# Sharing the low-part subtraction of weight units 4 to 14 between VectorE and GpSimd in a two-layer encoder kernel

## The chip, the cores and the metric

One core of one Trainium2 chip runs the whole kernel in one launch. The metric is the time of that launch in device microseconds: lower is better. Weights, inputs and constants start in HBM, and the result ends there.

## What is computed

Two layers (`DEPTH = 2`) of an encoder block on x of 256 tokens by 1024 channels, float32:

```
h = RMSNorm(x);  z = h @ W_in              # 1024 x 6656: q, k, v of A and B, pool channels, gates
A = grouped-query attention (8 query heads, 2 key heads, 64 wide), QK norm, axial rotary
B = dilated window attention (12 heads in 3 groups), QK norm, rotary
C = centred mean pooling of 4 channel groups, a linear map per group
x = x + W_o( sum_i sigmoid(gate_i) * P_i(branch_i) )
x = x + (silu(h2 @ W_gate) * (h2 @ W_up)) @ W_down,   h2 = RMSNorm(x),  inner width 2816
```

The kernel keeps nearly float32 precision in products of a reduced-precision float format: each operand is split in a high part (rounded) and a low part (the rest), and a product is hi*hi + lo*hi + hi*lo, three matmuls for each pair of tiles.

## The kernel before

**Weights in units.** All weights of a layer are laid out as a stream of 68 units (`UNITS`). A unit is 1 MB: four k-tiles of 128 rows (`UK = 4`) by 512 columns (`NC`). Units 0 to 25 are W_in, two units for each of 13 column chunks of z; then come the branch projections, W_o, and the feed-forward weights. Four slots (`RING`) of three buffers hold them: `w_raw` (as landed), `w_hi` and `w_lo`.

**A unit's way.** SyncE (line 447) loads unit u into slot u % 4 when TensorE has finished unit u - 4. ScalarE (`split`, line 589) copies `w_raw` to `w_hi`, which rounds it, and raises `unit_hi`. VectorE (`split`, line 752) subtracts, `w_lo = w_raw - w_hi`, over all four k-tiles in one instruction of 2048 columns (line 755), and raises `unit_lo`. Both do this for unit t + 2 at the start of their iteration t. Unit 0 of a layer is split tile by tile (lines 587 and 761).

**TensorE.** For each unit and each of two token tiles (m = 0, 1), `rows` (line 1022) runs eight matmuls with the high part, in pairs (activation high, line 1036, activation low, line 1038), and then four with the low part (line 1047). With m = 0 (`opening`) it waits for `unit_hi` before the first and for `unit_lo` before the low ones; m = 1 waits for neither. Between units and between the two token tiles stand transposes (line 1069), scores (lines 1131 and 1140) and products of probabilities and values (line 1163), by tables written by hand (`TURNS_BEFORE`, `TURNS_WITHIN`, `pair_at`). In unit 0 each high matmul pair and each low matmul has a wait of its own on its k-tile (`first_hi`, `first_lo`).

**VectorE around units 2 to 14.** Iteration t: the maxima of scores (line 868), if any; the split of unit t + 2 (line 755); the scaling of probabilities (line 891), if any; `norm_rotated` of the head region that was rotated one iteration earlier (line 862), which waits for GpSimd's head norms; then `rotate` (lines 830 to 854): the sums of squares for the region (line 830, `head_sums`), and the rotary products and sums. The transposes of queries and keys on TensorE wait for `rotated`, which line 862 raises: those ahead of unit 6 and within it for the first region (two instances of line 862, one per token tile), those ahead of unit 7 for the second, and so on.

**GpSimd around units 2 to 14.** Iteration t of the loop at line 553: `join_probs` (line 512) at t = 12, 14, ..., which waits for the probabilities' transposing DMA, and from the second pair on for TensorE's unit; `head_norm` (lines 485 and 487, a scaling and a power) for the regions of t, which waits for `head_sums`; the loads of gate biases (line 519) from t = 16 on. TensorE's products of line 1163 begin ahead of unit 13 and wait for `join_probs`. In the feed-forward part GpSimd splits hidden values in 16-bit halves and puts them together again (lines 530 and 539).

Of the kernel before, what the change touches and what calls it, by code (L numbers as in the profile page):

```python
# [16 lines left out]
F32 = mybir.dt.float32  # L17
# [3 lines left out]
ALU = mybir.AluOpType  # L21
# [11 lines left out]
UK = 4  # L33
# [8 lines left out]
RING = 4  # L42
# [10 lines left out]
UNITS = U_DOWN + 11  # L53
# [142 lines left out]
POOL_LINKS = 4 + TURNED  # L196


def splits_at(t, ahead=2):

    if t < 2:
        return {2: ([1], [2, 3]), 3: ([1, 2], [3])}[ahead][t]
    return [t + 2] if t + 2 < UNITS else []


def build(nc, x, stream, params, b_gate, eye, angles, pooling, mask, out):
# [3 lines left out]
    with ExitStack() as ctx:  # L210
        def sb(name, shape, dt=F32, to=ctx):
            return to.enter_context(nc.sbuf_tensor(name, shape, dt))

        def sem(name):
            return ctx.enter_context(nc.semaphore(name))
# [17 lines left out]
        w_hi = sb("w_hi", [P, RING, UK, NC], F32R)  # L233
        with ExitStack() as shared:
            w_raw = sb("w_raw", [P, RING, UK, NC], F32, shared)
        w_lo = sb("w_lo", [P, RING, UK, NC], F32R)
# [62 lines left out]
        unit_done = sem("unit_done")  # L299
        unit_hi = sem("unit_hi")  # L300
        unit_lo = sem("unit_lo")
        first_hi = sem("first_hi")
        first_lo = sem("first_lo")
        bank_full = [sem(f"bank_full{b}") for b in range(8)]
# [88 lines left out]
        def probs_room(i):  # L393

            if i < 8:
                return gates[:, i % 2, QK_W:QK_W + NC].bitcast(U16)
            return zqk[:, 1, 1024 + NC * (i % 2):1024 + NC * (i % 2) + NC].bitcast(U16)
# [66 lines left out]
        @block.gpsimd  # L464
        def _(pool):
            def load_gains(layer):
                pool.dma_start(par[:, 0:PR_GAIN], params_v[layer * P:layer * P + P, 0:PR_GAIN]
                               ).then_inc(gains_loaded, 16)

            def load_params(layer):  # L470
                pool.dma_start(par[:, PR_GAIN:PR_W], params_v[layer * P:layer * P + P, PR_GAIN:PR_W]
                               ).then_inc(params_loaded, 16)

            nc.gpsimd.memset(neg_half[:, :, :], -0.5).then_inc(half_ready, 1)
            pool.wait_ge(x1_loaded, 16)
            load_params(0)
            pool.dma_start(rope_c[:, :, :, :].rearrange("p k m d -> p (k m d)"), angles
                           ).then_inc(angles_loaded, 16)

            pool.dma_start(mask_f, mask).then_inc(mask_loaded, 16)  # L480
            pool.wait_ge(half_ready, 1)

            def power(lay, link, dst, src, mul, eps, signal):

                nc.gpsimd.tensor_scalar(dst[1], src, mul, eps, ALU.mult, ALU.add).then_inc(pchain, 1)
                pool.wait_ge(pchain, lay * POOL_LINKS + (link + 1))
                nc.gpsimd.tensor_tensor(dst[0], dst[1], dst[2], ALU.pow).then_inc(signal, 1)  # L487

            def x_norms(lay, which, link):
                pool.wait_ge(x_sums, lay * 8 + 4 * (which + 1))  # L490
                nc.gpsimd.tensor_tensor(sx[:, which, :], ssx[:, 0, :], ssx[:, 1, :], ALU.add  # L491
                                        ).then_inc(pchain, 1)
                pool.wait_ge(pchain, lay * POOL_LINKS + (link + 1))
                power(lay, link + 1, (rstd[:, which, :], sx[:, which, :], neg_half[:, 0, 0:MT]),
                      sx[:, which, :], 1.0 / D, EPS, x_norm)

            def head_norm(lay, n):

                (name, _, hs, first, _, _, _), m = REGIONS[n // MT], n % MT
                mul, eps = (1.0, HD * EPS) if name[2] == "q" else (1.0 / HD, EPS)  # L500
                pool.wait_ge(head_sums, lay * TURNED + (n + 1))
                h = slice(first, first + hs)
                power(lay, 2 + n, (rs[:, m, h], rs_in[:, m, h], neg_half[:, m, h]),
                      ss[:, m, h], mul, eps, head_norms)

            def join_probs(lay, t, i):

                pool.wait_ge(probs_turned[i % 2], 16 * (lay * PAIRS + i // 2 + 1))
                if i >= 2:
                    pool.wait_ge(unit_done, lay * UNITS + RING + t)  # L510
                both = probsT[:, i % 2, :].bitcast(U16).rearrange("p (t h) -> p h t", h=2)
                nc.gpsimd.tensor_copy(both, probs_room(i).rearrange("p (h t) -> p h t", h=2)  # L512
                                      ).then_inc(probs_joined, 1)

            def load_bias(lay, g):
                if g >= 2:
                    for m in range(MT):
                        wait_emptied(pool, lay, (f"z{GATE_CHUNK + g - 2}", m))
                pool.dma_start(bias_sb[:, g % 2, :],
                               gate_v[lay * 6 + g:lay * 6 + g + 1, :].to_broadcast([P, NC])  # L520
                               ).then_inc(bias_loaded[g % 2], 16)

            def hidden_halves(lay, i):

                b = i % 2
                for m in range(MT):
                    wait_emptied(pool, lay, (f"f{i}", m))
                both = hid[:, b, :, :].bitcast(U16).rearrange("p m (f h) -> p m f h", h=2)
                for h in range(2):
                    nc.gpsimd.tensor_copy(halves[:, b, :, h, :], both[:, :, :, h]).then_inc(halves_ready, 1)  # L530

            def hidden_whole(lay, i):

                b = i % 2
                uses = (FC + 1 - b) // 2
                pool.wait_ge(halves_turned[b], 16 * (lay * uses + i // 2 + 1))
                both = hT_raw[:, 2 * i:2 * i + 2, :].bitcast(U16).rearrange("p k (m t h) -> p k m t h", m=MT, h=2)
                for h in range(2):
                    nc.gpsimd.tensor_copy(both[:, :, :, :, h],  # L539
                                          turned[:, b, :, h, :, :].rearrange("p m k t -> p k m t")  # L540
                                          ).then_inc(raw_ready, 1)

            for lay in range(DEPTH):
                load_bias(lay, 0)
                load_bias(lay, 1)
                x_norms(lay, 0, 0)
                if lay == 0:

                    pool.wait_ge(mask_loaded, 16)
                    nc.gpsimd.tensor_copy(mask_sb[:, :], mask_f).then_inc(mask_ready, 1)  # L550
                    pool.dma_start(pool_mat[:, :, :, :].rearrange("p m g n -> p (m g n)"), pooling
                                   ).then_inc(pooling_loaded, 16)
                for t in range(U_A0):
                    p = pair_at(t, 3)
                    if p is not None:
                        join_probs(lay, t, 2 * p)
                        join_probs(lay, t, 2 * p + 1)
                    for n in range(TURNED):
                        if REGIONS[n // MT][-1][n % MT] == t:
                            head_norm(lay, n)  # L560
                    g, odd = divmod(t - 16, 2)
                    if 0 <= g < 4 and not odd:
                        load_bias(lay, g + 2)
                x_norms(lay, 1, 2 + TURNED)

                wait_lo(pool, lay, ("ffn_x", 3))
                load_gains(min(lay + 1, DEPTH - 1))
                load_params(min(lay + 1, DEPTH - 1))
                for i in range(FC):
                    hidden_halves(lay, i)  # L570
                    hidden_whole(lay, i)
# [168 lines left out]
        def _(dve):  # L740
# [10 lines left out]

            def split(lay, j):
                dve.wait_ge(unit_hi, lay * (UNITS - 1) + j)
                w = [a[:, j % RING, :, :].rearrange("p k n -> p (k n)") for a in (w_lo, w_raw, w_hi)]
                nc.vector.tensor_tensor(w[0], w[1], w[2].bitcast(F32), ALU.subtract).then_inc(unit_lo, 1)  # L755

            def split_first(lay):
# [179 lines left out]
            for lay in range(DEPTH):  # L937
# [3 lines left out]
                for t in range(UNITS):  # L941
                    p = pair_at(t, 0)
# [50 lines left out]
                    i, odd = divmod(t - U_FFN, 2)  # L993
# [25 lines left out]
        def _(pe):  # L1019
            pe.sem_inc(unit_done, RING)  # L1020

            def rows(lay, t, name, m, src, tiles, wk, first, final, opening=False, ready=None):
# [21 lines left out]
                for i, k in enumerate(tiles):  # L1044
                    if opening and not t:
                        pe.wait_ge(first_lo, lay * UK + (i + 1))
                    last = nc.tensor.matmul(o, src[0][:, k, tok], w_lo[:, slot, wk + i, :], start=False,  # L1047
                                            stop=final and i == len(tiles) - 1)
                if final:
# [134 lines left out]
            for lay in range(DEPTH):  # L1184
                for t in range(UNITS):
# [26 lines left out]
                    elif t < U_FFN:  # L1212
                        half, n = divmod(t - U_OUT, 2)
# [3 lines left out]
                    elif t < U_DOWN:  # L1217
                        i, half = divmod(t - U_FFN, 2)
# [121 lines left out]
```

## Time and profile before

| | |
|---|---|
| median of 3 runs | 822.84 us (822.7 to 823.5) |
| the profiled execution, whole | 823.74 us |
| its span, first to last instruction | 821.9 us |
| TensorE busy | 816.8 us, 99% |
| its weight loads, which overlap the matmuls | 667.4 us, 81% |
| VectorE busy | 574.0 us, 70% |
| ScalarE busy | 436.4 us, 53% |
| GpSimd busy | 239.3 us, 29% |
| moved by DMA | 165.76 MB, 202 GB/s in the mean |

PE is TensorE's matmul, PEld its weight load, DVE is VectorE, ACT ScalarE, POOL GpSimd, SP SyncE. All times are microseconds, those marked mean are nanoseconds. Matmuls overlap their neighbours, so the duration of one (0.39 us) is more than the distance between two starts (0.23 us). "Idle before" is an engine's idle time just ahead of a group, and behind it stands what ended most of it.

### The profile page before, as it was taken

To read this page: it belongs to the slowest core of one execution; us is meant where nothing else is said; L and a number is where in the kernel's file an instruction comes from. 1 tells how busy PE (TensorE), PEld (TensorE's weight loads), DVE (VectorE), ACT (ScalarE), POOL (GpSimd) and SP (SyncE) were. 2 spreads that over 40 slices of the span, in tenths; PEclk is the share of its full clock that TensorE was granted. 3 is DMA by queue.
4 is the path that set the end of the run, shared out by engine and by line. 5 is a ranking of instruction groups with operands and counts; after the bars stand their busy time and mean duration, and the time that the engine had idled before them with its cause. 6 is when DMAs were issued, how large, how long until landed. Compare 5 with 4: busy or idle time off the path is not lost.

```text
span 821.9 us, 9923 instructions
## 1 busy us (share of the span) xinstructions
PE 816.8 (99%) x3884; PEld 667.4 (81%) x3884; DVE 574.0 (70%) x688; ACT 436.4 (53%) x505; POOL 239.3 (29%) x206
## 2 busy tenths in 40 slices
PE   9999999999999999999999999999999999999998
PEld 7887778888888888888888877878888888888886
DVE  5999776667776767664379996677586767666552
ACT  6767755573364454543456686555734544444430
POOL 1342324230023444430023241524200444444200
PEclk9999999999999999999999999999999999999999
DMA  9756687685557676676455467677644566776661
GB/s 343 273 188 179 182 204 203 189 221 171 188 174 230 221 214 200 225 243 215 161 198 203 156 186 198 192 201 204 199 181 177 198 213 224 230 223 206 204 209 43
DMA packets 80142, 165.76 MB, mean 202 GB/s; under 512 B 59840, under 2 KB 60000, under 8 KB 62688
## 3 DMA queue, kind: packets, MB, share of 16 engines
q1 hardware_dynamic: 78176, 158.88, 61.3%
q0 software_dynamic: 1632, 6.18, 2.2%
q8 instruction: 31, 0.51, 0.3%
q10 hardware_dynamic: 288, 0.08, 0.0%
q14 instruction: 15, 0.12, 0.0%
HBM read 149.91 MB, written 1.05 MB: 184 GB/s over the span
## 4 chain that ended last, share of the span: by engine, by line
PE 98%; DMA 1%; DVE 0%; ACT 0%; SPq 0%; issue 0%
PE bank L1036 30%; PE bank L1038 30%; PE bank L1047 30%; PE bank L1069 2%; PE bank L1163 2%; PE bank L1140 1%; PE bank L1131 1%; PE bank L1104 1%; DMA x_sb<-in_x_dram 1%; PE bank L1110 0%; DVE w_lo L755 0%; PE bank L1173 0%; ACT w_hi L591 0%; ACT aT_hi L601 0%; DVE scratch L779 0%; DVE x_sb L931 0%
## 5 line engine op out<-in xcount | busy, mean ns | idle before, releaser
L755 DVE TENSOR_TENSOR w_lo<-w_raw,w_hi 128x2048 fp32r<-128x2048 f32 x134 | 317.8, 2374 | 97.5 <-ACT w_hi L591 97.1
L591 ACT ACTIVATE w_hi<-w_raw 128x2048 fp32r<-128x2048 f32 x134 | 256.3, 1915 | 155.5 <-DMA w_raw<-in_stream_dram 155.3
L1036 PE MATMUL bank<-w_hi,aT_hi 128*128 128x512 f32 x832 | 330.3, 397 | 0.0
L1038 PE MATMUL bank<-w_hi,aT_lo 128*128 128x512 f32 x832 | 324.7, 390 | 0.0
L1047 PE MATMUL bank<-w_lo,aT_hi 128*128 128x512 f32 x832 | 223.6, 391 | 0.1
L1036 PEld LDWEIGHTS bank<-w_hi,aT_hi 128*128 128x128 f32 x832 | 156.4, 188 | 37.3 <-issue 5.7
L1047 PEld LDWEIGHTS bank<-w_lo,aT_hi 128*128 128x128 f32 x832 | 155.6, 188 | 33.1 <-DVE w_lo L755 0.7
L1038 PEld LDWEIGHTS bank<-w_hi,aT_lo 128*128 128x128 f32 x832 | 156.6, 188 | 31.4
L539 POOL COPY hT_raw<-turned 128x512 uint16<-128x512 uint16 x44 | 35.6, 853 | 135.1 <-DMA turned<-halves 135.1
L530 POOL COPY halves<-hid 128x512 uint16<-128x512 uint16 x44 | 71.8, 1660 | 4.5 <-DVE hid L1008 4.5
L1036 PE MATMUL bank<-w_hi,hT_hi 128*128 128x512 f32 x176 | 68.7, 390 | 0.0
L1038 PE MATMUL bank<-w_hi,hT_lo 128*128 128x512 f32 x176 | 68.6, 390 | 0.0
L736 ACT ACTIVATE sg<-bank,rstd 128x256 f32<-128x256 f32 x44 | 20.8, 473 | 75.9 <-PE bank L1047 69.5
L512 POOL COPY probsT<-zqk 128x1024 uint16<-128x1024 uint16 x16 | 36.0, 2286 | 72.6 <-PE bank L1047 46.5
L491 POOL TENSOR_TENSOR sx<-ssx 128x2 f32<-128x2 f32 x4 | 4.0, 1007 | 167.4 <-ACT probsT L655 167.4
L1047 PE MATMUL bank<-w_lo,hT_hi 128*128 128x512 f32 x176 | 47.8, 390 | 0.0
L512 POOL COPY probsT<-gates 128x1024 uint16<-128x1024 uint16 x16 | 29.5, 1889 | 61.7 <-PE bank L1047 43.1
L1001 DVE SCALAR_TENSOR_TENSOR scratch<-bank,rstd,sg 128x256 f32<-128x256 f32 x44 | 21.2, 481 | 37.2 <-ACT sg L736 37.2
L1047 PEld LDWEIGHTS bank<-w_lo,hT_hi 128*128 128x128 f32 x176 | 33.0, 188 | 6.9
L1036 PEld LDWEIGHTS bank<-w_hi,hT_hi 128*128 128x128 f32 x176 | 33.0, 188 | 6.8
L1038 PEld LDWEIGHTS bank<-w_hi,hT_lo 128*128 128x128 f32 x176 | 33.1, 188 | 6.8
L487 POOL TENSOR_TENSOR rs<-rs_in,neg_half 128x8 f32<-128x8 f32 (+2 forms) x24 | 33.2, 1382 | 2.0
(98 smaller groups left out, 745.4 us busy)
## 6 DMA issues: line engine op xcount, KB each, us to landing
w_raw<-in_stream_dram SPq DMA_DIRECT2D x135, 1024.0 KB, 4.8
bias_sb<-in_b_gate_dram POOLq DMA_DIRECT2D x12, 256.0 KB, 3.5
par<-in_params_dram POOLq DMA_DIRECT2D x3, 384.0 KB, 3.5
w_raw<-in_stream_dram SPq DMA_DIRECT2D x4, 256.0 KB, 5.3
pool_mat<-in_pooling_dram POOLq DMA_DIRECT2D x1, 1024.0 KB, 7.5
out_dram<-x_sb SPq DMA_DIRECT2D x4, 256.0 KB, 4.2
x_sb<-in_x_dram SPq DMA_DIRECT2D x2, 256.0 KB, 4.1
x_sb<-in_x_dram SPq DMA_DIRECT2D x1, 512.0 KB, 6.3
```

Source lines behind the costliest of these rows:

```text
L487: nc.gpsimd.tensor_tensor(dst[0], dst[1], dst[2], ALU.pow).then_inc(signal, 1)
L512: nc.gpsimd.tensor_copy(both, probs_room(i).rearrange("p (h t) -> p h t", h=2)).then_inc(probs_joined, 1)
L530: nc.gpsimd.tensor_copy(halves[:, b, :, h, :], both[:, :, :, h]).then_inc(halves_ready, 1)
L539: nc.gpsimd.tensor_copy(both[:, :, :, :, h], turned[:, b, :, h, :, :].rearrange("p m k t -> p k m t")).then_inc(raw_ready, 1)
L591: nc.scalar.activation(w_hi[:, j % RING, :, :].rearrange("p k n -> p (k n)"), w_raw[:, j % RING, :, :].rearrange("p k n -> p (k n)"), ACT. ...
L736: nc.scalar.activation(sg[:, i % 2, m, :], B((f"f{i}", m))[:, 0:256], ACT.Sigmoid, scale=rstd[:, 1, m:m + 1]).then_inc(sig_done, 1)
L755: nc.vector.tensor_tensor(w[0], w[1], w[2].bitcast(F32), ALU.subtract).then_inc(unit_lo, 1)
L1001: made.append(link(nc.vector.scalar_tensor_tensor(scratch[:, 2 * NC + 256 * m:2 * NC + 256 * m + 256], B((f"f{i}", m))[:, 0:256], rstd[:, ...
L1036: nc.tensor.matmul(o, src[0][:, k, tok], w_hi[:, slot, wk + i, :], start=first and i == 0, stop=False)
L1038: nc.tensor.matmul(o, src[1][:, k, tok], w_hi[:, slot, wk + i, :], start=False, stop=False)
L1047: last = nc.tensor.matmul(o, src[0][:, k, tok], w_lo[:, slot, wk + i, :], start=False, stop=final and i == len(tiles) - 1)
L1069: return nc.tensor.transpose(b[:, at:at + P], src, ident[:, :])
```

## The change

For units 4 to 14 of each layer VectorE subtracts the first three k-tiles only, in one instruction of 1536 columns, and GpSimd subtracts the fourth, in one instruction of 512 columns, with a semaphore of its own, for which TensorE waits before the fourth low matmul of token tile 0. GpSimd's instruction for unit t + 2 stands in its iteration t behind `join_probs` and ahead of `head_norm`, and waits for `unit_hi`. All other units are as before.

```diff
+SHARED = range(4, 15)
+KEPT = UK - 1
...
+        last_tile_lo = sem("last_tile_lo")
...
+            def split_last_tile(lay, j):
+
+                pool.wait_ge(unit_hi, lay * (UNITS - 1) + j)
+                w = [a[:, j % RING, KEPT, :] for a in (w_lo, w_raw, w_hi)]
+                nc.gpsimd.tensor_tensor(w[0], w[1], w[2].bitcast(F32), ALU.subtract).then_inc(last_tile_lo, 1)
...
                     if p is not None:
                         join_probs(lay, t, 2 * p)
                         join_probs(lay, t, 2 * p + 1)
+                    if t + 2 in SHARED:
+                        split_last_tile(lay, t + 2)
                     for n in range(TURNED):
                         if REGIONS[n // MT][-1][n % MT] == t:
                             head_norm(lay, n)
...
             def split(lay, j):
                 dve.wait_ge(unit_hi, lay * (UNITS - 1) + j)
-                w = [a[:, j % RING, :, :].rearrange("p k n -> p (k n)") for a in (w_lo, w_raw, w_hi)]
+                k = KEPT if j in SHARED else UK
+                w = [a[:, j % RING, 0:k, :].rearrange("p k n -> p (k n)") for a in (w_lo, w_raw, w_hi)]
                 nc.vector.tensor_tensor(w[0], w[1], w[2].bitcast(F32), ALU.subtract).then_inc(unit_lo, 1)
...
                     if opening and not t:
                         pe.wait_ge(first_lo, lay * UK + (i + 1))
+                    if opening and t in SHARED and i == KEPT:
+                        pe.wait_ge(last_tile_lo, lay * len(SHARED) + SHARED.index(t) + 1)
                     last = nc.tensor.matmul(o, src[0][:, k, tok], w_lo[:, slot, wk + i, :], start=False,
                                             stop=final and i == len(tiles) - 1)
```

## Rows read from the trace of the kernel before

**Rows 1.** The page: busy time by engine, and the chain that ended last.
```profile
PE 816.8 (99%) x3884; PEld 667.4 (81%) x3884; DVE 574.0 (70%) x688; ACT 436.4 (53%) x505; POOL 239.3 (29%) x206
PE 98%; DMA 1%; DVE 0%; ACT 0%; SPq 0%; issue 0%
```

**Rows 2.** Waits of TensorE's weight loader: total us, times, longest us.
```profile
PEld bank L1163 <- POOL probsT L512: 1.1, 3, 0.4
...
PEld bank L1047 <- DVE w_lo L755: 0.7, 2, 0.6
```

**Rows 3.** TensorE by stretch: us, busy (instructions), granted clock, DMA share, GB/s.
```profile
26.80:87.30 60.50, 60.50 (x284) 1.00 0.58 198
431.00:491.00 60.00, 60.00 (x282) 1.00 0.56 184
```

**Rows 4.** All engines by stretch: us, PE, PEld, DVE, ACT, POOL, clock, DMA, GB/s.
```profile
26.80:62.20 35.40, 35.40 (x166) 29.05 (x164) 34.84 (x55) 22.11 (x28) 12.94 (x16) 1.00 0.55 204
431.50:466.30 34.80, 34.80 (x163) 28.51 (x162) 34.21 (x55) 22.16 (x29) 12.94 (x16) 1.00 0.51 182
```

**Rows 5.** VectorE's subtractions: one instance in time order (start, us), one group by line.
```profile
436.47 2.28 DVE L755 TENSOR_TENSOR w_lo<-w_raw,w_hi 128x2048 fp32r<-128x2048 f32 x1
...
L761 DVE TENSOR_TENSOR w_lo<-w_raw,w_hi 128x512 fp32r<-128x512 f32 x8 | 5.0, 684 | 0.0
```

**Rows 6.** GpSimd's groups by line: busy us, mean ns, idle before.
```profile
L530 POOL COPY halves<-hid 128x512 uint16<-128x512 uint16 x44 | 71.8, 1660 | 4.5 <-DVE hid L1008 4.5
L512 POOL COPY probsT<-zqk 128x1024 uint16<-128x1024 uint16 x16 | 36.0, 2286 | 72.6 <-PE bank L1047 46.5 <-DMA zqk<-qkT 26.1
...
L550 POOL CAST mask_sb<-gates 128x1024 bf16<-128x1024 f32 x1 | 1.0, 1026 | 0.0
```

**Rows 7.** Line 512 (ns: min/median/max), then both engines in time order from 124 us.
```profile
L512 POOL COPY probsT<-gates x16: 1357/1373/3391, 81.2 to 530.1; 128x1024 uint16<-128x1024 uint16 x16
...
124.93 4.65 POOL L512 COPY probsT<-gates 128x1024 uint16<-128x1024 uint16 x2 [9.94 <-DMA gates<-scratch]
...
125.30 3.08 DVE L755 TENSOR_TENSOR w_lo<-w_raw,w_hi 128x2048 fp32r<-128x2048 f32 x1
```

**Rows 8.** VectorE in time order: unit 10 (layer 0), first region and unit 10 (layer 1).
```profile
59.31 2.28 DVE L755 TENSOR_TENSOR w_lo<-w_raw,w_hi 128x2048 fp32r<-128x2048 f32 x1
...
444.19 0.68 DVE L862 TENSOR_TENSOR zqk<-zqk,rs 128x512 f32<-128x512 f32 x1
...
464.04 2.28 DVE L755 TENSOR_TENSOR w_lo<-w_raw,w_hi 128x2048 fp32r<-128x2048 f32 x1
```

**Rows 9.** TensorE in time order: low matmuls of units 4 and 10, first transposes, unit 10.
```profile
34.71 1.07 PE L1047 MATMUL bank<-w_lo,aT_hi 128*128 128x512 f32 x4
...
69.86 1.07 PE L1047 MATMUL bank<-w_lo,aT_hi 128*128 128x512 f32 x4
...
447.86 0.60 PE L1069 MATMUL bank<-ident,zqk 128*128 128x128 f32 x4
...
473.96 1.07 PE L1047 MATMUL bank<-w_lo,aT_hi 128*128 128x512 f32 x4
```

**Rows 10.** Time order: ScalarE's split of unit 4; GpSimd's head norm, first join; its use.
```profile
24.86 1.92 ACT L591 ACTIVATE w_hi<-w_raw 128x2048 fp32r<-128x2048 f32 x1 [0.65 <-DMA w_raw<-in_stream_dram]
...
52.22 1.69 POOL L487 TENSOR_TENSOR rs<-rs_in,neg_half 128x8 f32<-128x8 f32 x1
...
81.21 2.86 POOL L512 COPY probsT<-gates 128x1024 uint16<-128x1024 uint16 x2 [4.27 <-DMA gates<-scratch]
...
88.27 1.08 PE L1163 MATMUL bank<-probsT,zvu 128*64 128x256 f32 x8
```

**Rows 11.** TensorE in layer 1: high matmuls of unit 0, first low ones of unit 1.
```profile
415.09 0.39 PE L1036 MATMUL bank<-w_hi,aT_hi 128*128 128x512 f32 x1
415.32 0.39 PE L1038 MATMUL bank<-w_hi,aT_lo 128*128 128x512 f32 x1
...
422.42 1.10 PE L1047 MATMUL bank<-w_lo,aT_hi 128*128 128x512 f32 x4
```

## The prediction

> **What bounds the kernel now.** I read the page first. TensorE is busy 99% of the span, and the chain that ended last is 98% TensorE [rows 1]. VectorE, which makes the low parts of the weights, is busy 70% and holds 0% of that chain. The second view is who TensorE's weight loader waited for: in the whole execution it waited 0.7 us in two places for the low parts of line 755, and 1.1 us in three places for GpSimd's joined probabilities [rows 2]. The third view asks the same of the stretches that the change touches. Layer 1 runs 404.1 us behind layer 0 (69.86 and 473.96 us for the same matmul [rows 9]). In 60 us of either layer, in which the low parts of units 4 to 14 are made, TensorE is busy for every microsecond, and its granted clock is 1.00, the 2.4 GHz level [rows 3]. So in these units nothing upstream is late, and time can be won there only if TensorE itself went faster.
>
> The stretch has one other feature, which makes the edit tempting: for 35 us in each layer VectorE is busy 34.2 to 34.8 us, as full as TensorE, and GpSimd only 12.9 us [rows 4]. VectorE is saturated there and yet not late. The question is how large its lead is and what the edit does to it.
>
> **VectorE's saving.** The subtraction of four k-tiles takes 2.28 us in an undisturbed instance, that of one tile 0.68 us (line 761) [rows 5]. Three more tiles cost 1.60 us, 0.53 us each, so three tiles take 1.75 us and the edit frees 0.53 us per unit, 22 x 0.53 = 11.7 us of VectorE in all. Worth to the time: nothing, by [rows 3].
>
> **GpSimd's new work.** The trace shows no large two-input operation on GpSimd. From below: the cast of 128x1024 f32 elements took 1.03 us, so 512 elements of one input some 0.5 us. From above: the mean of 2.29 us for a copy of 128x1024 16-bit elements, a mean that holds times spent blocked; between them lies 1.66 us for the copies of 128x512 [rows 6]. I take 1.03 us, because two inputs of 512 f32 elements are as many elements read as the cast reads, and the cast is the nearest row in type. The 22 subtractions put 23 us on an engine with that room.
>
> The Trainium skill (GPSIMD Engine Reference, section 3.1) gives 4497 ns for GpSimd and 2293 ns for VectorE for an f32 two-input operation of 2048 columns; a quarter of the former would be an estimate of 1.12 us. For VectorE the trace agrees (2.28 us); for GpSimd no row shows it.
>
> **The two engines disturb each other.** At 124.93 us GpSimd begins two copies of 128x1024 which together take 4.65 us; alone one takes 1.36 us. VectorE's subtraction, begun at 125.30, takes 3.08 in place of 2.28 us, about the rest of the first copy longer; and the second copy lasts as if it had waited for the subtraction to end [rows 7]. So I charge a full block: each subtraction of GpSimd costs VectorE its whole duration d. VectorE's balance per unit is then not -0.53 but d - 0.53, that is +0.50 us at d = 1.03. The edit would load the engine that it means to relieve. The Trainium skill (SBUF — State Buffer, "Who interferes with whom") states just this against the change: a VectorE instruction with two SBUF inputs and a GpSimd instruction that reads SBUF exclude one another for the whole of whichever came first. The trace agrees, by the 3.08 us.
>
> **Does VectorE's loss reach TensorE?** I set each result of VectorE against its use, counting the splits before it [rows 8, 9].
> - Rotated queries for the transposes ahead of unit 6, layer 1: done at 444.19 + 0.68 = 444.87, used at 447.86. Lead 3.0 us, the smallest, after three splits (units 4, 5, 6). Loss 3 x 0.50 = 1.5 us.
> - Low part of unit 10, layer 1: done at 464.04 + 2.28 = 466.32, used at 473.96. Lead 7.6 us, after seven splits. Loss 3.5 us. In layer 0 the lead is 69.86 - (59.31 + 2.28) = 8.3 us.
>
> Nothing arrives late. The lead is used up from d = 0.53 + 3.0/3 = 1.53 us for the transposes, and from 0.53 + 7.6/7 = 1.62 us for unit 10. At d = 1.66 the transposes would be late by 3 x 1.13 - 3.0 = 0.4 us, once.
>
> **GpSimd's queue.** The subtraction of unit t + 2 stands in iteration t behind the joining of probabilities and ahead of the head norms of t, and waits for the high part. Behind that wait are only head norms whose sums VectorE makes after it has itself waited for the same high part, so the wait adds nothing; the duration does, up to 1.03 us plus one blocked instruction of 1.75. A head norm (1.69 us for its power) is used only after VectorE's rotation steps and its next split, and by operands that have the leads above. The fourth tile's own deadline is easy: unit 4's high part is done at 24.86 + 1.92 = 26.78, so the tile is ready, with one block, by 26.78 + 1.75 + 1.03 = 29.6, against some 35.4 us, when the fourth low matmul is due. The first joining (81.21 + 2.86 = 84.07, used at 88.27) stands ahead of unit 14's tile [rows 10]. No DMA issue is moved: GpSimd's bias loads come from iteration 16 on, and SyncE still loads a slot after TensorE's unit, which now includes the wait for both parts.
>
> **TensorE's extra waits.** 22 waits, one before the fourth low matmul of token tile 0. Behind each stands the whole matmul stream. The nearest rows for a met wait in the middle of a run are the high matmuls of unit 0 in layer 1, each tile with its own wait: starts 0.22 to 0.23 us apart, the ordinary pace. I take 0. From above: four low matmuls ahead of which a wait did bite took 1.10 instead of 1.07 us, hence 22 x 0.03 = 0.7 us [rows 11]. A gain is excluded, since a wait only adds.
>
> **Sum.** Saving 0, blocking 0 (hidden by leads of 3.0 us and more), GpSimd's queue 0, waits 0 (0 to 0.7). The profiled execution took 823.74 us, of which 821.9 are the span; it stands 0.9 us or 0.1% over the median of 822.84, and the sum against it leaves 823.7. For the median of runs I forecast 822.8 us.
>
> **Rivals.**
> *A. The block eats the lead (slower).* GpSimd's subtraction takes over 1.53 us and VectorE's losses add up between units 4 and 10, where it has no idle time [rows 4]. TensorE then waits first at the transposes ahead of unit 6, then for unit 10's low part. At d = 2.29 the loss per unit is 1.76: layer 1 pays 7 x 1.76 - 7.6 = 4.7 us in all, layer 0, with its lead of 8.3, 4.0 us; together 8.7, so 831.5 us. To be over 0.2% slower, d has to be about 1.78 (two layers, 14 x 1.25 = 17.5 less 15.9). For it: VectorE is full, and copies of this mean length exist. Against it: those spans hold blocked time, which I already charge; an undisturbed copy of 1024 elements takes 1.36 us.
> *B. A gain through VectorE (faster).* The blocks fall on moments when VectorE is not reading two operands, it runs 0.53 us earlier per unit, and joined probabilities arrive sooner. All of TensorE's waits for low parts and joined probabilities together are 1.8 us [rows 2]; half of it would give 821.9 us. Against it: the joins wait for transposing DMAs and TensorE's own units, not for the subtractions, and none of the waits for low parts lies in units 4 to 14.
> *C. The waits cost more than met waits do here.* 0.7 us as above, 823.5 us: still no change.
> The diff does what it says: the range holds 11 units and the wait covers every use of the fourth tile, since token tile 1 comes after tile 0.
>
> **How the numbers follow.** Forecast 0.85, A 0.06, C 0.06, B 0.03. About 0.2% (1.6 us) is what a measurement can tell from no change. A counts as slower, save that its mildest form stays below; B mostly stays within 0.2%. That makes faster 0.02, same 0.92, slower 0.06. The range: from below 822.84 less half a microsecond for the spread of the runs shown (822.7 to 823.5) and a small part of B, 822.3; from above 822.84 + 0.7 (waits) + 0.4 (d = 1.66) and the spread again, 824.1. A's full form is left out.
>
> **What would show it.** Right: TensorE busy for the whole of both 60 us stretches; VectorE's split of units 4 to 14 at 1.75 us where undisturbed and up to 2.8 where blocked; 22 subtractions on GpSimd of about 1.0 us, longer where blocked; the loader's waits still near 0.7 and 1.1 us. VectorE's sum over the window falls or rises by a few microseconds with no effect on the end. Wrong: waits of TensorE at line 1069 for VectorE, or at line 1047 for VectorE or GpSimd, between 34 and 100 us or 438 and 504 us; or starts of the fourth low matmul more than 0.23 us after the third.

## The result, and the profile after

The changed kernel takes 828.5 us (median of 4 runs, 826.85 to 829.68) against 823.17 us before (median of 4 runs): a ratio of 1.0063, with a 95% interval of 1.0043 to 1.0082. That is 5.3 us slower, where I had forecast no change. The profiled execution took 826.85 us, its span is 825.0 us; it is the fastest of the four.

In the changed kernel the same lines stand 5 to 16 lines further down: 755 is now 769, 862 is 876, 868 is 882, 1036 is 1050, 1047 is 1063, 1163 is 1179. Lines 628 and 722 of ScalarE (exponentials, evacuation of z) are 641 and 735, GpSimd's joining of line 512 is 523, and its new subtraction is line 515.

First the page, to be set beside [rows 1]:

```profile
PE 816.0 (99%) x3884; PEld 665.3 (81%) x3884; DVE 577.8 (70%) x688; ACT 436.1 (53%) x505; POOL 295.7 (36%) x228
PE 81%; DVE 10%; issue 4%; ACT 2%; DMA 1%; POOL 1%; SPq 0%; DVEq 0%; ACTq 0%
```

TensorE works as long as before, 816 us, but the chain that ended last is no longer TensorE's alone: a tenth of it now runs through VectorE. VectorE's total rose by 3.8 us, although its shared splits became shorter. The two stretches of [rows 3] now hold idle time of TensorE, 1.96 and 1.62 us:

```profile
26.80:87.30 60.50, 58.54 (x274) 1.00 0.58 198
431.00:491.00 60.00, 58.38 (x271) 1.00 0.56 189
```

What TensorE waited for (total us, times, longest us), to be set beside [rows 2]. The last row is the weight loader's:

```profile
PE bank L1050 <- ACT zvu L735: 3.6, 2, 2.0
...
PE bank L1063 <- DVE w_lo L769: 0.2, 1, 0.2
...
PEld bank L1179 <- POOL probsT L523: 0.8, 2, 0.5
```

The waits for low parts and for joined probabilities are as small as they were. New is one wait in each layer, of the first high matmul of unit 12 for ScalarE's evacuation of z chunk 5. Chunks 5 and 6 of z both use the banks 0 and 1, so unit 12, which begins chunk 6, needs them emptied right after unit 11 has filled them. In the time order of the changed kernel (start, us; VectorE, ScalarE, TensorE):

```profile
78.34 1.28 DVE L882 TENSOR_REDUCE neg_max<-bank 128x2 f32<-128x512 f32 x2
...
79.06 0.47 ACT L641 ACTIVATE probs<-bank,neg_max 128x256 f32<-128x256 f32 x1 [3.01 <-DVE neg_max L882]
...
81.35 1.29 ACT L735 ACTIVATE zvu<-bank,rstd 128x512 f32<-128x512 f32 x2
...
79.09 1.07 PE L1063 MATMUL bank<-w_lo,aT_hi 128*128 128x512 f32 x4
82.12 0.50 PE L1050 MATMUL bank<-w_hi,aT_hi 128*128 128x512 f32 x1 [1.96 <-ACT zvu L735]
```

And the same places in the kernel before, which I had not read:

```profile
76.81 1.28 DVE L868 TENSOR_REDUCE neg_max<-bank 128x2 f32<-128x512 f32 x2
...
77.53 0.47 ACT L628 ACTIVATE probs<-bank,neg_max 128x256 f32<-128x256 f32 x1 [2.10 <-DVE neg_max L868]
...
79.82 0.71 ACT L722 ACTIVATE zvu<-bank,rstd 128x512 f32<-128x512 f32 x1
...
80.27 1.07 PE L1047 MATMUL bank<-w_lo,aT_hi 128*128 128x512 f32 x4
81.18 0.39 PE L1036 MATMUL bank<-w_hi,aT_hi 128*128 128x512 f32 x1
```

Read them as a chain. ScalarE's exponentials wait for VectorE's score maxima; the evacuation of chunk 5 stands behind the exponentials in ScalarE's queue; unit 12 needs the bank. In the kernel before the first evacuation ended at 79.82 + 0.71 = 80.53, 0.65 us before unit 12 began. In the kernel after, VectorE's maxima come 1.53 us later, and TensorE in this execution had started 1.18 us earlier (the low matmuls of unit 11's second token tile at 79.09 instead of 80.27): 2.7 us more of lateness against a lead of 0.65, hence a wait of 2 us. From these low matmuls to the next ones (84.06) 4.97 us pass, before it was 82.99 - 80.27 = 2.72: 2.25 us lost in layer 0. In layer 1 it is 4.65 us, 1.93 lost. Together 4.2 us; less the earlier start of 1.18 that makes the 3.1 us by which the span grew, within 0.1.

(That TensorE was early in this execution makes the wait longer, not the end later: unit 12 starts when the bank is free.)

Why VectorE is late is seen in the starts of its splits, each time before and after. Unit 5: 31.73 and 31.44; unit 6: 37.26 and 37.54; unit 7: 42.29 and 43.14; unit 8: 48.19 and 49.62; unit 9: 53.78 and 55.77; unit 10: 59.31 and 61.85. It falls back by 0.57 us a unit. One period of it in the changed kernel, GpSimd's row behind:

```profile
37.54 1.75 DVE L769 TENSOR_TENSOR w_lo<-w_raw,w_hi 128x1536 fp32r<-128x1536 f32 x1
39.21 1.78 DVE L876 TENSOR_TENSOR zqk<-zqk,rs 128x512 f32<-128x512 f32 x1
...
37.63 2.81 POOL L515 TENSOR_TENSOR w_lo<-w_raw,w_hi 128x512 fp32r<-128x512 f32 x1
```

The two subtractions become ready together. VectorE's comes first, at its undisturbed 1.75 us, and GpSimd's, on record from 37.63, ends at 40.44, 1.15 us after it. In that time VectorE's next two-input instruction stands still: the product with the head norms takes 1.78 instead of 0.68 us [rows 8]. So a unit gives VectorE 0.53 and takes 1.10. Two of the nine shared splits ahead of these maxima cost nothing. Behind that of unit 4 stands a reduction with one input, which keeps its 0.67 us, and only the rest of the block, 0.51 us, falls on the products after it. And GpSimd's subtraction of unit 11 runs while VectorE takes score maxima from PSUM, 1.27 us as ever. That such an overlap costs neither engine anything is seen at 78 us:

```profile
78.34 1.28 DVE L882 TENSOR_REDUCE neg_max<-bank 128x2 f32<-128x512 f32 x2
78.44 1.29 POOL L515 TENSOR_TENSOR w_lo<-w_raw,w_hi 128x512 fp32r<-128x512 f32 x1
```

### The profile page after: what moved, and what is told of

It is laid out like the page before. It is cut to its first block, busy times and chain, and to the rows that moved or that the text cites. A ratio compares the mean times of both kernels' runs of the same rounds, so it can differ in the third digit from the quotient of the medians.

```text
span 825.0 us, 9945 instructions
## 1 busy us (share of the span) xinstructions
PE 816.0 (99%) x3884; PEld 665.3 (81%) x3884; DVE 577.8 (70%) x688; ACT 436.1 (53%) x505; POOL 295.7 (36%) x228
## 4 chain that ended last, share of the span: by engine, by line
PE 81%; DVE 10%; issue 4%; ACT 2%; DMA 1%; POOL 1%; SPq 0%; DVEq 0%; ACTq 0%
PE bank L1050 25%; PE bank L1052 25%; PE bank L1063 25%; DVE zqk L876 3%; PE bank L1179 2%; PE bank L1085 2%; DVE scratch L859 1%; DVE zqk L863 1%; DMA w_raw<-in_stream_dram 1%; DVE ss L844 1%; PE bank L1156 1%; DVE zqk L868 1%; PE bank L1120 1%; DVE w_lo L769 1%; PE bank L1147 1%
## 5 line engine op out<-in xcount | busy, mean ns | idle before, releaser
L769 DVE TENSOR_TENSOR w_lo<-w_raw,w_hi 128x2048 fp32r<-128x2048 f32 (+1 forms) x134 | 303.4, 2266 | 100.0 <-ACT w_hi L604 99.6
L550 POOL COPY hT_raw<-turned 128x512 uint16<-128x512 uint16 x44 | 37.6, 901 | 133.4 <-DMA turned<-halves 133.4
L515 POOL TENSOR_TENSOR w_lo<-w_raw,w_hi 128x512 fp32r<-128x512 f32 x22 | 53.2, 2424 | 6.2 <-ACT w_hi L604 6.2
L523 POOL COPY probsT<-gates 128x1024 uint16<-128x1024 uint16 x16 | 31.3, 2000 | 53.2 <-PE bank L1063 42.3
```

Source lines behind the costliest of these rows:

```text
L515: nc.gpsimd.tensor_tensor(w[0], w[1], w[2].bitcast(F32), ALU.subtract).then_inc(last_tile_lo, 1)
L550: nc.gpsimd.tensor_copy(both[:, :, :, :, h], turned[:, b, :, h, :, :].rearrange("p m k t -> p k m t")).then_inc(raw_ready, 1)
```

## The experiments

Three theories. **S**, late bank: the chain just read. **W**: the 22 added waits on TensorE cost time of themselves. **G**: GpSimd's own work (fourth tile, head norms, joined probabilities) comes late. Each kernel is timed beside the kernel before on one chip; the medians of the latter were 823.3 to 823.6 us.

**1. The change once more (a1_repeat).** No edit.

> The changed kernel itself once more. Three theories are open. S (late bank): GpSimd's subtractions block VectorE, its score maxima of unit 11 come late, ScalarE's evacuation of z chunk 5 stands behind the exponentials of these scores, and TensorE's unit 12 waits about 2 us in each layer for that bank. W (waits): the 22 added waits of TensorE cost time wherever they stand. G (GpSimd late): the fourth tile or the head norms come late. S expects about 826.9 us in runs whose granted clock is 1.000, and 1.6 us more where the mean clock is 0.998, as in three of the four runs so far, hence a median of 827 to 829; the profile should show the wait ahead of unit 12, at 1.6 to 2.0 us, in both layers again. W and G expect the same total, and no such single wait.

828.12 us, ratio 1.0049 (1.0031 to 1.0066). The traced execution took 827.37 us and has the same two waits, 3.1 us together, the longest 1.7. The six times fall in two groups, 826.80, 826.84, 827.37 at a mean granted clock of 1.000 and 828.87, 829.30, 829.36 at 0.998; experiment 9 shows why.

**2. The waits without the work (b1_waits_only).**

```diff
...
-                nc.gpsimd.tensor_tensor(w[0], w[1], w[2].bitcast(F32), ALU.subtract).then_inc(last_tile_lo, 1)
...
+                nc.gpsimd.memset(gap[:, n:n + 2], 0.0).then_inc(last_tile_lo, 1)
...
-                k = KEPT if j in SHARED else UK
+                k = UK
```

> VectorE subtracts all four tiles again; GpSimd, in the same place of its queue and behind the same wait, writes two columns of an unused tile and raises the semaphore, and TensorE keeps its 22 extra waits. S expects 823.2 us, no change (within 0.7 us), since nothing of GpSimd's reads long in the buffer. W expects the whole loss of some 5 us, 828 us. G expects no change too, so this run tells W from the others.

823.91 us, ratio 0.9998 (0.9989 to 1.0008): no change. W falls, and with it the thought that GpSimd's wait for the high part holds up anything behind it.

**3. Only units 12 to 14 (g1_late_units).** `SHARED = range(12, 15)`.

> The change for units 12 to 14 alone. S: only unit 12's subtraction (iteration 10) comes before the maxima of iteration 11, a block costs VectorE about 0.6 us net, and VectorE was idle for 1.05 us ahead of its split of unit 12, so the maxima are not late; no wait ahead of unit 12; 823.2 us, within 0.5 us. W: 6 of 22 waits, 3/11 of 5.3 us, hence 824.6 us. G, if the joins of iterations 12 and 14 or the fourth tile were late: 3/11 or more of the loss, with a wait of the loader at the products with the values or at the fourth low matmul.

823.98 us, ratio 1.0002 (0.9991 to 1.0012). TensorE has no wait ahead of unit 12 in this trace (its weight loader waits 0.24 and 0.25 us). A loss in proportion to the shared units, 3/11 of the 0.49 to 0.63% measured for the whole change, would be a ratio of 1.0013 to 1.0017, which lies outside the interval, but not by much.

**4. Only units 4 to 7 (l1_early_units).** `SHARED = range(4, 8)`.

> The change for units 4 to 7 alone. S: unit 4's block cost nothing in the changed kernel's trace and each later one 0.57 us, so VectorE falls 1.7 us behind, and its idle times before the maxima of iteration 11 (0.38 and 1.05 us in the kernel before) take up 1.4 of it; 0.3 us of lateness against a lead of 0.65: no wait, or one of a few tenths where TensorE started early: 823.2 to 824.2 us. A loss simply proportional to the number of shared units gives 4/11 of 5 us, 825 us.

824.21 us, ratio 1.0008 (0.9999 to 1.0017): not told apart from no change, while the 825 us of a proportional loss lie outside. The loader's waits ahead of unit 12 are 0.7 us together in the traced execution, the fastest of the eleven, so this is about where the lead is used up. With seven more units the loss is 4.5 to 5.3 us: it sets in when the lead is gone, and does not grow from the first unit on.

**5. Another bank for chunk 5 (d1_banks, and d2_banks_before for the kernel before).** Chunk 5 goes to the banks 2 and 3, chunk 4 to 0 and 1.

```diff
-        pair(2 if c in (0, 2, 4) else 0, f"z{c}")
+        pair(2 if c in (0, 2, 5) else 0, f"z{c}")
```

> The change as it is, and z chunk 5 moved to the banks 2 and 3, z chunk 4 to 0 and 1, so that unit 12 (z chunk 6, banks 0 and 1) no longer needs chunk 5 evacuated; its bank was freed two units before. S expects both waits ahead of unit 12 to vanish and the time to fall to about 823.2 us, up to 824.5 if the next late thing shows (the joined probabilities ahead of unit 13, or chunk 4 behind chunk 3 on one pair of banks, whose lead I read as 1.3 us), although VectorE is as late as in the changed kernel. W and G expect 828 us as before, since nothing that they speak of is touched.

> The kernel before with the bank plan of the fourth run (chunk 5 on banks 2 and 3, chunk 4 on 0 and 1). TensorE had no wait there, so all theories expect 823.2 us within 0.3 us: this is the reference for the run with the change and the plan together.

With the change: 825.17 us, ratio 1.0017 (1.0007 to 1.0027). Without it: 823.51 us, ratio 1.0002 (0.9993 to 1.0011). The wait ahead of unit 12 is gone and two thirds of the loss with it, but more is left than the 824.5 us that I expected at most. The trace, of the slowest of the eleven executions (826.97 us), shows where it went (TensorE in time order, layers 0 and 1):

```profile
96.26 0.50 PE L1050 MATMUL bank<-w_hi,aT_hi 128*128 128x512 f32 x1 [1.54 <-ACT zvu L735]
...
501.53 0.50 PE L1050 MATMUL bank<-w_hi,aT_hi 128*128 128x512 f32 x1 [0.48 <-ACT zvu L735]
```

These are the first matmuls of unit 14, which wait for chunk 6 in the same way: behind the exponentials of iteration 13. Most likely this is because TensorE no longer stood still ahead of unit 12, 1.96 and 1.62 us in the changed kernel's own profile, which there put off its need of the next bank by as much. TensorE also waits 0.7 us in two places for the joined probabilities here. No run of the change removes both waits by banks alone.

**6. The evacuation ahead of the exponentials (k1_evac_first).** Everything of the change stays; ScalarE alone is reordered, in iterations 11 and 13.

```diff
-                    if p is not None:
+                    if p is not None and t not in (11, 13):
                         softmax_exp(lay, 2 * p)
                         softmax_exp(lay, 2 * p + 1)
...
                             free(last, (f"z{c}", m))
+                    if t in (11, 13):
+                        softmax_exp(lay, 2 * p)
+                        softmax_exp(lay, 2 * p + 1)
```

> The change as it is, with one move on ScalarE: in iterations 11 and 13 the evacuation of the z chunk (5 and 6) stands ahead of the exponentials of that iteration's scores instead of behind them. Nothing on VectorE, GpSimd or TensorE is edited. S: the evacuation no longer waits for VectorE's late maxima, so neither unit 12 nor unit 14 waits for its bank: 823.2 to 824 us, against 828 without the move, unless the later exponentials delay the joined probabilities. If a wait of 2 us ahead of unit 12 stays, the path through the maxima is wrong.

823.39 us, ratio 0.9999 (0.9990 to 1.0008). The whole loss is gone. VectorE is, if anything, later than in the changed kernel, and TensorE does not stop (VectorE, ScalarE and TensorE in time order; VectorE's and TensorE's line numbers are 3 higher than in the changed kernel):

```profile
79.53 1.28 DVE L885 TENSOR_REDUCE neg_max<-bank 128x2 f32<-128x512 f32 x2
...
78.21 0.68 ACT L735 ACTIVATE zvu<-bank,rstd 128x512 f32<-128x512 f32 x1
...
79.36 1.07 PE L1066 MATMUL bank<-w_lo,aT_hi 128*128 128x512 f32 x4
80.27 0.39 PE L1053 MATMUL bank<-w_hi,aT_hi 128*128 128x512 f32 x1
```

The maxima start 1.19 us later than in the changed kernel, and unit 12 still follows unit 11 without a gap. So VectorE's lateness reached TensorE only by the order on ScalarE. It also answers G: GpSimd's work is the same as in the changed kernel, and what it delays on GpSimd itself costs nothing. The move was not timed on the kernel before; TensorE has no wait there that it could take away.

**7. The lateness without the sharing (f1_act_delay).** The kernel before, with five small copies ahead of the evacuation of chunk 5.

```diff
+DELAYS = 5
...
+                        if c == 5:
+                            for _ in range(DELAYS):
+                                nc.scalar.activation(gap[:, 0:256], x_sb[:, 0, 0:256], ACT.Copy).then_inc(delayed, 1)
+                                n_delays[0] += 1
+                                act.wait_ge(delayed, n_delays[0])
```

> The kernel before, with no sharing, and five copies of 256 columns, each waited for, on ScalarE ahead of the evacuation of z chunk 5 in each layer: some 2.8 us of delay by my sum (0.47 us plus about 0.1 each). S, in which only the lateness of this evacuation matters and the lead before is 0.65 us, expects a wait of about 2.1 us ahead of unit 12 in each layer, a span 4 to 4.5 us longer, some runs at a mean clock of 0.998, and 827 to 829 us, like the changed kernel, without any work on GpSimd. W and G expect 823.2 us, or only what ScalarE's later splits would cost.

826.59 us (826.04 to 827.43), ratio 1.0043 (1.0029 to 1.0056). This is below the 827 to 829 us that I expected, and none of the five runs is near 829. The five copies took 2.23 us instead of 2.8, and TensorE waits 1.50 us ahead of unit 12 in each layer, not 2.1:

```profile
79.17 2.23 ACT L709 ACTIVATE align_gap<-x_sb 128x256 f32<-128x256 f32 x5
...
82.17 0.50 PE L1043 MATMUL bank<-w_hi,aT_hi 128*128 128x512 f32 x1 [1.50 <-ACT zvu L729]
...
488.06 0.50 PE L1043 MATMUL bank<-w_hi,aT_hi 128*128 128x512 f32 x1 [1.50 <-ACT zvu L729]
```

So a late bank of that size makes a loss of 3.3 us by itself, on a kernel where GpSimd does nothing new.

**8. What blocks VectorE (c1_write_only and h1_no_saving).** In the first, GpSimd's subtraction becomes `memset(w_lo[:, j % RING, KEPT, :].bitcast(F32), 0.0)`: the fourth tile's low part is left out of the product. In the second, VectorE keeps all four tiles, and GpSimd besides subtracts 512 columns of the high part from themselves and writes 16-bit values to an unused tile.

> As the change, but GpSimd writes zeros over the fourth tile's low part (512 columns) in place of the subtraction, reading nothing; the low part of one tile in four of units 4 to 14 is left out of the product. VectorE keeps its saving of 0.53 us per unit. S with blocking by GpSimd's reads expects VectorE's instructions at their undisturbed durations (1.75 us for the split, 0.68 for the head norms' product), no wait ahead of unit 12, 823.2 us. If GpSimd's writing blocks VectorE as well, the durations rise by up to half a microsecond and a part of the wait remains. W expects 828 us.

> VectorE subtracts all four tiles, and GpSimd in addition subtracts 512 columns of the high part from themselves into an unused tile of 16-bit values, at the same places: the block without the saving. S: VectorE loses 0.53 us more per unit than in the changed kernel. Nine splits stand before the maxima of iteration 11, so they come up to 4.8 us later in each layer, and so does unit 12: up to 9.5 us over the changed kernel, 833 to 838 us. W and G, in which VectorE's saving plays no part, expect 828 us.

Writing only: 823.04 us, ratio 1.0000 (0.9991 to 1.0009). The product with the head norms, by line with the mean in ns, in this kernel and then in the changed one:

```profile
L875 DVE TENSOR_TENSOR zqk<-zqk,rs 128x512 f32<-128x512 f32 x12 | 8.2, 684 | 0.0
```

```profile
L876 DVE TENSOR_TENSOR zqk<-zqk,rs 128x512 f32<-128x512 f32 x12 | 21.4, 1783 | 0.0
```

The zeros are written while VectorE's split runs, and neither is longer for it:

```profile
31.92 1.75 DVE L768 TENSOR_TENSOR w_lo<-w_raw,w_hi 128x1536 fp32r<-128x1536 f32 x1
33.59 0.68 DVE L875 TENSOR_TENSOR zqk<-zqk,rs 128x512 f32<-128x512 f32 x1
...
32.77 0.52 POOL L514 MEMSET w_lo<- 128x512 f32 x1
```

A GpSimd instruction that writes 512 columns and reads none does not slow VectorE at all (684 ns), one that reads two operands costs it 1.10 us. The Trainium skill (SBUF — State Buffer, "Who interferes with whom") says just that: a VectorE instruction with two SBUF inputs contends with a GpSimd instruction that reads, not with one that only writes. The trace agrees.

The block without the saving: 837.2 us, ratio 1.0166 (1.0152 to 1.0180), in the range that S expected, where W and G stayed at 828. The waits ahead of unit 12 grow to 5.31 and 4.45 us. The block is not quite that of the change, though. This subtraction takes GpSimd 1.03 us undisturbed instead of 1.29, and it stops VectorE's product for 0.85 us instead of 1.10:

```profile
41.37 1.53 DVE L879 TENSOR_TENSOR zqk<-zqk,rs 128x512 f32<-128x512 f32 x1
...
82.27 1.04 POOL L518 TENSOR_TENSOR align_gap<-w_hi 128x512 bf16<-128x512 f32 x1
```

VectorE's splits of units 5 to 10 fall back by 0.84 us each, not by the 1.10 that I had reckoned with, against 0.57 in the changed kernel. So what counts is VectorE's balance of blocks and savings, at the same 22 places and with the same 22 waits.

**9. Two more traces of the change (a2_repeat, a3_repeat).** No edit.

> The changed kernel once more, for a trace. Its runs so far fall in two groups, about 826.9 and about 829 us, and the listed mean clock is 1.000 in one of the first group, 0.998 in the others. In a run of the second group I expect TensorE's granted clock at 1.2 GHz for some microseconds right after one of the two waits ahead of unit 12, as the run with the 5.3 us wait shows it; in a run of the first, none.

> The same as the run before it, a second chance to catch a trace with the lower clock: TensorE at 1.2 GHz for some microseconds after one of the waits, and a total near 829 us; otherwise 827 us and full clock.

829.17 and 829.03 us, both of the second group. TensorE by stretch (us, busy and instructions, granted clock, DMA share, GB/s), around unit 12 of layer 0, first for the changed kernel's own profile (826.85 us), then for a2_repeat:

```profile
78.00:82.00 4.00, 2.16 (x10) 1.00 0.91 185
82.00:86.00 4.00, 3.88 (x19) 1.00 0.52 217
86.00:90.00 4.00, 4.00 (x25) 1.00 0.18 20
```

```profile
78.00:82.00 4.00, 2.45 (x11) 1.00 0.87 166
82.00:86.00 4.00, 2.92 (x7) 0.59 0.60 246
86.00:90.00 4.00, 4.00 (x21) 0.98 0.00 0
```

and in its time order:

```profile
83.08 0.80 PE L1050 MATMUL bank<-w_hi,aT_hi 128*128 128x512 f32 x1 [2.63 <-ACT zvu L735]
...
84.10 0.63 PE L1050 MATMUL bank<-w_hi,aT_hi 128*128 128x512 f32 x1
84.53 0.63 PE L1052 MATMUL bank<-w_hi,aT_lo 128*128 128x512 f32 x1
...
86.42 1.09 PE L1063 MATMUL bank<-w_lo,aT_hi 128*128 128x512 f32 x4
```

After the wait the matmuls start 0.43 us apart instead of 0.23: the granted clock is at 1.2 GHz, and is back at 2.4 shortly after 86 us. From 83.08 to the low matmuls takes 3.34 us, where the first group's execution needs 84.06 - 82.12 = 1.94: the lower clock costs 1.4 us here, and the longer wait (2.63 against 1.96 us) 0.7. That is 2.1 of the 2.3 us between these two executions. In a3_repeat the wait is only 1.97 us and the clock falls all the same: 3.31 us from unit 12 (82.58) to its low matmuls (85.89). In both the wait of layer 1 (1.65 and 1.68 us) is followed by full clock.

## Why the prediction was wrong

**The bound now** was read rightly: TensorE had no wait in these stretches, nothing was to be gained, and nothing was.

**VectorE's saving**: 1.75 us for three tiles, as worked out.

**GpSimd's work**: I took d = 1.03 us. The shortest of the 22 instances has 1.29 us on record, their mean is 2.42, and they cost VectorE 1.10. The records of most hold the time in which GpSimd was itself blocked. The whole duration was not charged either: 1.29 us stop VectorE for 1.10, and the 1.03 of h1_no_saving for 0.85. A d too low by 0.26 and a block too high by about 0.2 nearly cancel, and that the block came out close to 1.03 is in part luck.

**The block**: right in kind and nearly in size. I charged d - 0.53 = 0.50 us per unit, and 0.57 was measured where the next instruction of VectorE has two SBUF inputs. That VectorE would end up later for the change is what happened.

**"Does VectorE's loss reach TensorE?"** is the step that failed. I listed the low parts and the rotated queries and called 3.0 us the smallest lead. The one at unit 12 was 0.65 us, in both layers, on a path that goes on behind VectorE's results: score maxima, ScalarE's exponentials, and behind these, only by the order of its queue, the evacuation that frees unit 12's bank. The maxima of iteration 11 came 1.53 us later, which is well over that. Against the loss stand the pauses in which VectorE catches up, in the kernel before:

```profile
62.58 1.29 DVE L868 TENSOR_REDUCE neg_max<-bank 128x2 f32<-128x512 f32 x2 [0.38 <-PE bank L1131]
...
71.28 2.29 DVE L755 TENSOR_TENSOR w_lo<-w_raw,w_hi 128x2048 fp32r<-128x2048 f32 x1 [1.05 <-ACT w_hi L591]
...
475.38 2.29 DVE L755 TENSOR_TENSOR w_lo<-w_raw,w_hi 128x2048 fp32r<-128x2048 f32 x1 [0.89 <-ACT w_hi L591]
```

By the same kind of sum as in the prediction, seven splits cost d - 0.53 each (5 to 10 and 12), that of unit 4 costs nothing, and that of unit 11 gives its 0.53 back. The lead is then used up at d = 0.53 + (0.65 + 1.43 + 0.53)/7 = 0.90 us in layer 0 and at 0.53 + (0.65 + 0.89 + 0.53)/7 = 0.83 us in layer 1, not at 1.53. My own d of 1.03 lies above both, by 0.9 and 1.4 us of lateness: the right list would have forecast a loss of some 2.3 us. The rest of what was measured comes, as far as the traces show, from the larger block and, in most executions, from the lower clock. The edge of every unit where TensorE needs a PSUM bank had to be on the list, each with the last instruction that frees it.

**GpSimd's queue and TensorE's waits** cost nothing, as forecast (experiments 2 and 6).

**The rivals.** A had the right mechanism, VectorE's losses adding up until they exceed a lead, but at the wrong place and with a threshold of 1.53 us instead of 0.83 to 0.90; I gave it 0.06. B and C did not happen. What I named as signs of being wrong, waits at the transposes or the low matmuls, did not appear either: the wait is at the first high matmul of unit 12. The lower clock in some executions was in no case of mine; it belongs to the price of a wait of 2 us here, 1.4 us in a2_repeat.

No version beats the kernel before. Experiment 6 makes the change harmless, at 823.39 us, and widens the lead at unit 12 to 1.38 us, but TensorE has no idle time there that anything could win.

## What to carry to other kernels

Before giving an engine more work, or another engine work that blocks it, list the leads of all who wait behind it: also those who stand behind its consumer in that consumer's queue, and the PSUM bank that is needed next. A wait that is met by half a microsecond is in no view of waits; it has to be worked out from two timelines, end of the release against start of the use. And moving a fourth of a VectorE subtraction to GpSimd does not relieve VectorE when both read two SBUF operands at the same time: here 0.53 us were freed and 1.10 blocked, per unit.

## What the runs showed of the hardware that was not expected

- A wait of TensorE costs more than its length when the clock falls during it or just behind it. With waits of 2.63 us (a2_repeat), 1.97 us (a3_repeat) and 4.45 us (h1_no_saving, layer 1) the granted clock was at 1.2 GHz for 3.4 us, with 5.31 us (h1_no_saving, layer 0) for 6.8 us, part of it still in the wait. With 1.96 us (the changed kernel's profile) it stayed at 2.4 GHz, and so it did with 1.45 to 1.68 us (a1_repeat, and layer 1 of all four traces of the change) and with 1.50 us twice (f1_act_delay). The twelve executions of the changed kernel therefore fall in two groups, 826.8 to 827.4 and 828.5 to 829.7 us; the second was traced twice.
- GpSimd and VectorE held each other up where GpSimd's instruction read and VectorE's had two SBUF inputs, and not otherwise: zeros written over 512 columns took GpSimd 0.52 us and VectorE nothing, and beside GpSimd's subtraction score maxima from PSUM (1.28 us for two) and a reduction of one input (0.67 us) kept their times.
- The recorded span of GpSimd's instruction includes the time in which it is itself blocked: 1.29 us undisturbed and 2.8 us in the usual case. What it takes from VectorE is less than its undisturbed span, 1.10 of 1.29 us and 0.85 of 1.03.
